# Layer norms: VectorE adds the scaled residual into PSUM sums that are still open

## The reference, cut to what matters

```
h = layer_norm(ALPHA * h + mix(h))     # mix: an SSD mixer (layer 0), latent attention (layer 1)
h = layer_norm(ALPHA * h + conv_ffn(h))
layer_norm(x) = (x - mean) * rsqrt(var + 1e-5) * g + b
```

## Time and profile before

| what | us |
|---|---|
| median of 3 runs (lowest, highest) | 1258.52 (1258.48, 1260.17) |
| span of the profiled execution | 1257.2 |
| TensorE busy in it | 1242.1 |
| VectorE busy in it | 932.5 |
| ScalarE busy in it | 684.2 |

### The profile page before, as it was taken

One profiled execution on the slowest core, in us unless ns is written; L12 is line 12 of the kernel. 1 busy time (PEld: TensorE's weight loads), 2 busy tenths in 40 slices (PEclk: granted clock), 3 DMA queues, 4 the chain that ended last, 5 costly groups with the idle time before them and its releaser, 6 DMA issues. The chain is left out here.

```text
span 1257.2 us, 18334 instructions
## 1 busy us (share of the span) xinstructions
PE 1242.1 (99%) x7514; PEld 1102.9 (88%) x7514; DVE 932.5 (74%) x1292; ACT 684.2 (54%) x872; POOL 68.2 (5%) x93
## 2 busy tenths in 40 slices
PE   9999999999999999999999999999999999999997
PEld 8878999989988888889998888888888888888886
DVE  6676857875456666577997998788888868788877
ACT  6654444343553444455777655466655574566652
POOL 2000000100000000000003331000000000000000
PEclk9999999999999999999999999999999999999999
DMA  9664545656435665647656654655554744655551
GB/s 294 219 184 144 185 143 188 214 186 209 168 101 170 199 194 178 197 138 219 185 168 210 203 191 151 217 185 201 184 186 138 231 134 134 201 194 179 197 194 41
DMA packets 162595, 227.97 MB, mean 181 GB/s; under 512 B 7853, under 2 KB 123825, under 8 KB 162384
## 3 DMA queue, kind: packets, MB, share of 16 engines
q1 hardware_dynamic: 159392, 216.68, 53.5%
q0 software_dynamic: 2816, 9.52, 2.3%
q10 hardware_dynamic: 304, 0.59, 0.1%
HBM read 225.68 MB, written 1.10 MB: 180 GB/s over the span
## 5 line engine op out<-in xcount | busy, mean ns | idle before, releaser
L1310 DVE TENSOR_TENSOR wlo<-raw,whi 128x2048 fp32r<-128x2048 f32 (+3 forms) x185 | 415.9, 2260 | 113.9 <-ACT whi L830 112.8
L830 ACT ACTIVATE whi<-raw 128x2048 fp32r<-128x2048 f32 (+3 forms) x185 | 345.9, 1883 | 16.0 <-DMA raw<-in_w_xkv 6.1
L2159 PE MATMUL psum<-h_both,whi 128*128 128x512 f32 x714 | 254.7, 396 | 0.0
L2158 PE MATMUL psum<-h_both,wlo 128*128 128x256 f32 x714 | 199.4, 279 | 0.3 <-DVE h_both L1364 0.3
L2125 PE MATMUL psum<-h_both,whi 128*128 128x256 f32 x688 | 195.9, 285 | 0.0
L2127 PE MATMUL psum<-h_both,wlo 128*128 128x256 f32 x688 | 194.6, 283 | 0.0
L2126 PE MATMUL psum<-h_both,whi 128*128 128x256 f32 x688 | 194.6, 283 | 0.0
L2125 PE MATMUL psum<-whi,r_hi 128*128 128x512 f32 x446 | 176.6, 396 | 0.0
L2127 PE MATMUL psum<-whi,r_lo 128*128 128x512 f32 x446 | 173.9, 390 | 0.0
L2126 PE MATMUL psum<-wlo,r_hi 128*128 128x512 f32 x446 | 173.8, 390 | 0.0
L2159 PEld LDWEIGHTS psum<-h_both,whi 128*128 128x128 f32 x714 | 134.0, 188 | 27.6
(11 more groups left out here) (350 smaller groups left out, 1807.1 us busy)
## 6 DMA issues: line engine op xcount, KB each, us to landing
raw<-in_ffn_up SPq DMA_DIRECT2D x40, 1024.0 KB, 5.1
raw<-in_w_in SPq DMA_DIRECT2D x31, 1024.0 KB, 5.8
raw<-in_ssd_in_proj SPq DMA_DIRECT2D x22, 1024.0 KB, 5.4
raw<-in_ffn_down SPq DMA_DIRECT2D x22, 1024.0 KB, 4.9
raw<-in_w_up SPq DMA_DIRECT2D x16, 1024.0 KB, 5.6
raw<-in_w_down SPq DMA_DIRECT2D x16, 1024.0 KB, 4.9
raw<-in_w_xkv SPq DMA_DIRECT2D x8, 1024.0 KB, 5.2
raw<-in_ssd_out_proj SPq DMA_DIRECT2D x8, 1024.0 KB, 5.2
```

The lines of the kernel that those rows point to most:

```text
L830: A(whi[u % SLOTS][:, 0:kt * n], raw[u % SLOTS][:, 0:kt * n], ACT.Copy).then_inc(hi_split, 1)
L1310: V.tensor_tensor(wlo[s][:, 0:kt * n], raw[s][:, 0:kt * n], whi[s][:, 0:kt * n].bitcast(F32), ALU.subtract).then_inc(lo_split, 1)
L2158: M(b[:, 0:T], w_lo_k, h_hi[:, k, :], start=False, stop=False)
L2159: return M(b[:, :], w_hi_k, h_both[:, :, k, :], start=False, stop=k == kt - 1)
```

## The change

The addition `ALPHA * xn` leaves the layer norm and becomes `add_residual`, which VectorE runs on a bank whose sum is not finished. TensorE waits for it (new semaphore `residual_in`) before it adds further to that bank.

- `so`: VectorE adds into the two banks of c0 once unit `so` (2, 0) has been used, then clears the pads of the feed-forward, then adds into those of c1 once `so` (2, 1) has been used. This stands after its last half of `lo` in the SSD part. TensorE waits in `last_two`, ahead of each bank's twelve matmuls.
- both feed-forwards: in group 9, after `ffn_taps` of half x, VectorE adds into the two banks of tile t = x, once fd 7 has been used. TensorE waits in fd 8, ahead of each bank.
- `ao`: VectorE adds c0 after step 9 of attention and a `lo`, c1 after step 10. TensorE waits in `last_two`.
- the flags `stop` of the units ahead are set, since VectorE touches the bank between; the later matmuls go on without `start`.

The core of the diff:

```diff
+            def add_residual(name, unit, places):
+                dve.wait_ge(unit_used, at[unit] + 1)
+                for c, t in places:
+                    b = bank[use[name(c, t)][0]][:, :]
+                    V.scalar_tensor_tensor(b, xn[:, t, halves[c]], ALPHA, b, ALU.mult, ALU.add).then_inc(residual_in, 1)
...
                     if rms:
                         chain(V.scalar_tensor_tensor(b, b, inv_ms[:, t:t + 1], x_, ALU.mult, ALU.add))
-                    else:
-                        chain(V.scalar_tensor_tensor(b, x_, alpha, b, ALU.mult, ALU.add))
                     mark(V.bn_stats(bn[:, t, c, :], b))
...
             for i in range(2):
                 lo_half(i)
+            so_sum = lambda c, t: ("so", c, t)
+            add_residual(so_sum, ("so", 2, 0), [(0, 0), (0, 1)])
...
                         ffn_taps(layer, g, x)
+                        if g == FFN_GROUPS - 2:
+                            add_residual(lambda c, t: ("ffn", layer, c, t), ("fd", layer, FFN_GROUPS - 4), [(0, x), (1, x)])
...
             ffn_pads()
+            add_residual(so_sum, ("so", 2, 1), [(1, 0), (1, 1)])
             lo()
-            layer_norm(lambda c, t: ("so", c, t), 3, lo_name="h5")
+            layer_norm(so_sum, 3, lo_name="h5")
...
             attend(9)
             lo()
+            add_residual(ao_sum, ("ao", 0, 0), [(0, 0), (0, 1)])
             attend(10)
+            add_residual(ao_sum, ("ao", 0, 1), [(1, 0), (1, 1)])
...
+            def residual_after(n):
+                pe.wait_ge(residual_in, residuals[0] + n)
...
+            def residual_first(inner):
+                def before(t, c, k):
+                    if k == 0:
+                        residual_after(2 * c + t + 1)
+                    inner(t, c, k)
+                return before
...
-                            last_two([at[("so", q, c)] for c in range(2)], r_hi, r_lo, 4, so_banks, first_tile("h5"))
+                            last_two([at[("so", q, c)] for c in range(2)], r_hi, r_lo, 4, so_banks, residual_first(first_tile("h5")))
...
-                        wide_unit(at[("fd", layer, g)], r_hi, r_lo, 2 * (g % 4), banks, g == 0, False)
+                        wide_unit(at[("fd", layer, g)], r_hi, r_lo, 2 * (g % 4), banks, g == 0, g == FFN_GROUPS - 4,
+                                  before=(lambda t, c: residual_after(2 * t + c + 1)) if g == FFN_GROUPS - 3 else None)
```

More of the change, by code:

```diff
@@ L620, in build @@
         low_out = sem("low_out")
+        residual_in = sem("residual_in")
         dt_sum, dt_log, dta_ready, cum_row = sem("dt_sum"), sem("dt_log"), sem("dta_ready"), sem("cum_row")
@@ L1446, in residual, with layer_norm @@
                             after_tile()
-            def layer_norm(name, uses, alpha=ALPHA, lo_name=None, rms=False, piece=None):
+            def add_residual(name, unit, places):
[3 more added lines that the diff above has]
+                    V.scalar_tensor_tensor(b, xn[:, t, halves[c]], ALPHA, b, ALU.mult, ALU.add).then_inc(residual_in, 1)
+            def layer_norm(name, uses, lo_name=None, rms=False, piece=None):
                 def add(c, t):
@@ L2098, in _ @@
             lo()
+            ao_sum = lambda c, t: ("ao", c, t)
+            add_residual(ao_sum, ("ao", 0, 0), [(0, 0), (0, 1)])
             attend(10)
+            add_residual(ao_sum, ("ao", 0, 1), [(1, 0), (1, 1)])
             lo()
@@ L2102, in _ @@
             ffn_pads()
-            layer_norm(lambda c, t: ("ao", c, t), 5, lo_name="h7")
+            layer_norm(ao_sum, 5, lo_name="h7")
             ffn(1)
@@ L2110, in _ @@
             M = nc.tensor.matmul
-            halves_normed = [0]
+            halves_normed, residuals = [0], [0]
+            def residual_after(n):
+                pe.wait_ge(residual_in, residuals[0] + n)
             def claim(key):
@@ L2121, in fill, with three @@
                 return filled[use[key][0]]
[L2123 to L2127, removed]
+            def three(o, a_hi, a_lo, b_hi, b_lo, start, stop_, resumed=False):
+                M(o, a_hi, b_hi, start=start, stop=False, skip_group_check=resumed)
+                M(o, a_hi, b_lo, start=False, stop=False, skip_group_check=resumed)
+                return M(o, a_lo, b_hi, start=False, stop=stop_, skip_group_check=resumed)
             def weights(u):
@@ L2187, in a_unit, with wide_unit @@
                 last.then_inc(unit_used, 1)
-            def wide_unit(u, x_hi_, x_lo_, tile0, banks, first, final, summed=False):
+            def wide_unit(u, x_hi_, x_lo_, tile0, banks, first, final, summed=False, before=None):
                 w_hi, w_lo, kt, _ = weights(u)
@@ L2193, in wide_unit @@
                     for c in range(2):
+                        if before is not None:
+                            before(t, c)
                         for k in range(kt):
@@ L2196, in wide_unit @@
                             last = three(banks[c][t][:, :], x_hi_[:, tile0 + k, ts], x_lo_[:, tile0 + k, ts], w_hi[:, k, cs], w_lo[:, k, cs],
-                                         first and k == 0, final and k == kt - 1)
+                                         first and k == 0, final and k == kt - 1, before is not None)
                         if summed and (t, c) != (NT - 1, 1):
@@ L2211, in last_two, with last_two_wide @@
                             last = three(banks[c][t][:, :], x_hi_[:, tile0 + k, ts], x_lo_[:, tile0 + k, ts], w_hi[:, k, :], w_lo[:, k, :],
-                                         False, k == kt - 1)
+                                         False, k == kt - 1, True)
                         last.then_inc(bank_summed if t == 0 else unit_used, 1)
-            def last_two_wide(us, ready, x_hi_, x_lo_, tiles, banks, before):
+            def last_two_wide(us, ready, x_hi_, x_lo_, tiles, banks, before, resumed):
                 for t in range(NT):
@@ L2227, in last_two_wide @@
                                 last = three(banks[c][t][:, :], x_hi_[:, tiles[i] + k, ts], x_lo_[:, tiles[i] + k, ts], w_hi[:, k, cs], w_lo[:, k, cs],
-                                             False, (i, k) == (1, kt - 1))
+                                             False, (i, k) == (1, kt - 1), resumed)
                             if (t, c, i) == (1, 1, 0):
@@ L2581, in _ @@
             last_two_wide([at[("down", g)] for g in pair], lambda i: pe.wait_ge(up_lo, pair[i] + 1), r_hi, r_lo,
-                          [2 * (g % 3) for g in pair], mlp_banks, first_tile("h4"))
+                          [2 * (g % 3) for g in pair], mlp_banks, first_tile("h4"), False)
             def lead(name, us, first_key, back_keys):
@@ L2768, in _ @@
                         if k == 0:
-                            last_two([at[("so", q, c)] for c in range(2)], r_hi, r_lo, 4, so_banks, first_tile("h5"))
+                            last_two([at[("so", q, c)] for c in range(2)], r_hi, r_lo, 4, so_banks, residual_first(first_tile("h5")))
                         continue
-                    a_unit(at[("so", q, k)], r_hi, r_lo, 4 * (q % 2), so_banks[k], q == 0, False,
+                    a_unit(at[("so", q, k)], r_hi, r_lo, 4 * (q % 2), so_banks[k], q == 0, q == 2,
                            between=lambda n: ssd_step(SSD_PER_UNIT * u + n))
@@ L2791, in ffn @@
                         pe.wait_ge(f_lo, 11 * layer + g + 1)
-                        wide_unit(at[("fd", layer, g)], r_hi, r_lo, 2 * (g % 4), banks, g == 0, False)
+                        wide_unit(at[("fd", layer, g)], r_hi, r_lo, 2 * (g % 4), banks, g == 0, g == FFN_GROUPS - 4,
+                                  before=(lambda t, c: residual_after(2 * t + c + 1)) if g == FFN_GROUPS - 3 else None)
+                residuals[0] += 4
                 pair = (FFN_GROUPS - 2, FFN_GROUPS - 1)
                 last_two_wide([at[("fd", layer, g)] for g in pair], lambda i: pe.wait_ge(f_lo, 11 * layer + pair[i] + 1), r_hi, r_lo,
-                              [2 * (g % 4) for g in pair], banks, before_last)
+                              [2 * (g % 4) for g in pair], banks, before_last, True)
+            residuals[0] += 4
             ffn(0, "h5", first_tile("h6"))
@@ L2949, in attend_at @@
                 return between
+            ao_before = residual_first(first_tile("h7"))
             def before_second(t, c, k):
@@ L2953, in before_second @@
                     wait_drained(pe, ("mo", 2 + k // 2))
-                first_tile("h7")(t, c, k)
+                ao_before(t, c, k)
             ao = [[claim(("ao", c, t)) for t in range(NT)] for c in range(2)]
-            a_unit(at[("ao", 0, 0)], r_hi, r_lo, 4, ao[0], True, False, ready=mo_ready, between=attend_at(7))
-            a_unit(at[("ao", 0, 1)], r_hi, r_lo, 4, ao[1], True, False, between=attend_at(9))
+            a_unit(at[("ao", 0, 0)], r_hi, r_lo, 4, ao[0], True, True, ready=mo_ready, between=attend_at(7))
+            a_unit(at[("ao", 0, 1)], r_hi, r_lo, 4, ao[1], True, True, between=attend_at(9))
```

(1 more changed line is left out.)

## The result

The changed kernel takes 1262.26 us (median of 20 runs, 1260.57 to 1264.0); the kernel before, on the same chip, 1258.89 (1258.25 to 1260.9). The ratio is 1.0022 with a 95% interval of 1.0016 to 1.0029: slower, by 3.4 us in the medians. The forecast was 1261.3, with a range of 1258.9 to 1264.0.

A forecast was written before the change was run, and what follows sets the result against it. TensorE was taken as the bound, VectorE mattering only where TensorE waits and at the end. Net terms +1.77 (h5), +1.69 (h6), -0.56 (h7), -0.17 (feed-forward 1, end) gave 1258.52 + 2.73 = 1261.3 us, range 1258.9 to 1264.0.

The forecast's parts named there:

- the sum: Net over the whole kernel, 1.77 + 1.69 - 0.56 - 0.17 = +2.73 us, giving 1261.3 us.
- three signs of being wrong: No TensorE stop at `so`, a pause in feed-forward 0 under 2 us, or a clock fall behind a pause.
- What bounds the kernel: TensorE, busy 1242.1 of 1257.2 us; VectorE's work counts only where TensorE waits for it and at the end.
- Part 1: Additions leaving the four layer norms win 0.58 us in h5, 0.83 in h6, 0.56 in h7, 1.02 at the end.
- Part 2: At `so`, TensorE pauses 2.35 us before the first bank of `last_two`; h5 nets +1.77 us.
- Part 3: In feed-forward 0, four additions delay `r_lo` of group 10 by 2.64 us; TensorE pauses 2.52, h6 nets +1.69.
- Part 4: At `ao`, the additions fall into VectorE's idle time and add nothing; h7 nets -0.56 us.
- Part 5: In feed-forward 1, TensorE pauses 0.85 us for `r_lo` of group 10; with 1.02 gained at the end, nets -0.17.
- rival C: Twelve matmuls behind each of two long pauses run at 1.2 GHz, 2.7 us more each: +8.1, 1266.7 us; chance 0.06.
- Rivals B and D: B: VectorE absorbs the additions, -2.99 us, 1255.5, chance 0.06. D: one long pause fails to come, 1258.8, chance 0.16.

The follow-up runs named there:

- e3: Kernel before with the change at `ao` only, additions elsewhere left in the layer norm; 1258.33 us, ratio 0.9995.
- e5: Changed kernel with all four additions of `so` ahead of VectorE's last two halves of `lo`; 1259.98 us.
- e8: Changed kernel with `so` additions ahead of the last two `lo` halves and feed-forward additions in groups 5 and 7, ahead of the taps; 1256.32 us.
- e6: Changed kernel with the feed-forwards' additions moved to groups 5 and 7, behind the taps; 1265.60 us, ratio 1.0051.
- e9: e8 with the c0 additions of `so` between VectorE's last two halves of `lo`; 1257.38 us, ratio 0.9988.
- e2: Kernel before with the change in the two feed-forwards only; 1259.86 us, ratio 1.0007.
- e4: Changed kernel with the two c0 additions of `so` between VectorE's last two halves of `lo`; 1259.83 us.
- e1: Kernel before with the change at `so` only; 1262.15 us, ratio 1.0022.
- e10: Changed kernel with only the feed-forwards' additions moved, to groups 5 and 7 ahead of the taps; 1260.02 us, ratio 1.0007.
- e7: Changed kernel with `so` additions ahead of the last two `lo` halves and feed-forward additions in groups 5 and 7, behind the taps; 1261.82 us, ratio 1.0018.

## Why the prediction was right, and where its terms were off

The direction was right, and so was the mechanism of the pauses. That the size came so near, +3.4 where the sum said +2.7, is in part luck. The nine executions without a fall of the clock are at +2.0 and the eleven with one at +4.0; the sum lies between the two, too high by its pairs of additions and too low by the fall that it left out. Two of the prediction's three signs of being wrong also came true: the pause of feed-forward 0 is under 2 us (+1.9 by the shift), and the clock fell behind a pause.

- **What bounds the kernel; a pause of TensorE is the price.** Right. But for the eight matmuls at the low clock and the end, every difference between the traces is a place where TensorE waits or no longer waits for VectorE. The additions themselves are as many as before (VectorE busy 932.5 and 930.7 us).
- **Part 1, what is removed.** Right for h6 (-0.84; 1.02 less three quarters of 0.227 is 0.85, where the sum took 0.83) and the end (-1.05, forecast -1.02). For h5 and h7 the transposes stopped waiting as said (-0.56 and -0.55), but 0.37 came back at once in each: the matmul behind the last transpose needs the low part of the third transposed half, and TensorE, now earlier, waits for that. In the trace of the changed kernel the last transpose of h5 begins at 799.21 and the next matmul 0.99 later, of which 0.37 is new by the comparison above. The profile puts the wait down to "issue"; that it is for VectorE's low part is read from the times: VectorE's row begins at 799.40 and lasts 0.69, so it ends 0.11 before the matmul starts. I had asked what is late next after the first stall and not after the second. e3 shows the same steps at h7, alone.

```profile
799.21 0.60 PE L2259 MATMUL psum<-cst,xn 128*128 128x128 f32 x4
799.40 0.69 DVE L1345 TENSOR_TENSOR h_both<-psum,h_both 128x512 fp32r<-128x512 f32 x1 [0.47 <-ACT h_both L847]
800.20 0.47 PE L2143 MATMUL psum<-whi,h_both 128*128 128x512 f32 x1 [0.39 <-issue]
```

- **Part 2, `so`.** The pause was right to 0.01 us. e5 shows that it is only the place in VectorE's queue: the same four additions, begun 2.3 us earlier against TensorE's time, cost less than 0.2 us.
- **Part 3, feed-forward 0.** Mechanism right, size off: `r_lo` of group 10 came 2.10 us later relative to TensorE's time, not 2.64. An addition moves what follows by less than its length. With the first pair of additions behind the taps the next `lo` begins 2.91 us after the taps' start (948.21 to 951.12), before 1.80 (944.43 to 946.23): 1.11 for the pair. With the second pair the product begins 2.91 after the taps' start (955.29 to 958.20), before 1.90 (950.41 to 952.31): 1.01. Together they are 2.12, where I had put 2.64.
- **Part 4, `ao`.** Right in that TensorE waits for nothing there; -0.35 instead of -0.56, for the reason given under part 1.
- **Part 5, feed-forward 1.** Pause 0.41, not 0.85; the same mis-sized pairs, 2.12 instead of 2.64, account for the difference to within 0.1.
- **The clock, rival C at 0.06.** This is the term that the forecast left out. It is not a fixed price but a chance: the clock fell in eleven of the twenty runs (by their times and clocks), and it cost 1.7 us in the profiled one. Two errors partly cancelled: without a fall the change costs 1260.87 - 1258.89 = +2.0 us where the sum said +2.7; with one, +4.0. By the price that I had derived, 2.7 us for twelve matmuls, the fall was smaller, since only eight matmuls ran at the low level. The trace of before had been read too boldly: a clock of 1.00 between 5 and 10 us did not show that a pause is harmless, since the longest gap there is 1.2 us. Nor was it so that this trace shows no fall anywhere. Behind TensorE's last matmul the granted clock is 1.00 up to 1254 and 0.50 from there to the end, where no matmul pays for it; the window over this stretch has 0.78:

```profile
1249.90:1257.20 7.30, 0.04 (x1) 0.00 (x0) 4.76 (x9) 0.00 (x0) 0.54 (x1) 0.78 0.38 144
```

The rule of the Trainium skill (TensorE: Matmul & The Clock Gate, Why this matters for your kernels) that idle gaps between bursts throttle TensorE was the better guide. These traces bear it out in kind but not in length: the gaps that it warns of are longer than the two here, TensorE's wait of 2.2 us at `so` and of 1.8 in feed-forward 0, so read strictly it would have let both pass.

- **Rivals B and D** are out for the changed kernel: both long pauses came.

The numbers leave +2.0 (no fall) against a sum of the measured steps of about +2.2; that 0.2 is within what single executions scatter (before: 1258.25 to 1260.9).

One question stays open: why the clock falls behind a pause in some executions and not in others. All that the runs show is the count for each kind of pause. These counts go by the two groups of times; the mean clock alone can't tell a fall, since it also takes in the low stretch at the end, and 0.998 stands with quick runs too (1256.03 in e8). With 17 of 98 runs of the kernel before in an upper group, some upper runs of the other kernels may also have another cause than their pause.

## What to carry to other kernels

- Moving work to an engine's idle time needs two checks at the new place: what stands behind it in that engine's queue, and when the other engine asks for the result. Here the same sixteen additions cost +3.4 us in one arrangement, +6.8 in another (e6) and won 2.5 in a third (e8).
- If the consumer's next step lies right behind the step from which the producer's queue is fed, nothing put behind that point in the queue can be in time; put it ahead.
- A pause of the matrix engine can cost more than its length, and only some of the executions show it. Look at the times and the granted clock of every run, not at one profile.

## What the runs showed of the hardware

- With no long pause (e8) or one of 1.2 us (e9) none of eleven runs is in an upper group. With the pause of about 2.0 us in feed-forward 0 and none above 1.2 elsewhere, three of eleven (e2), four of eleven (e4) and seven of eleven (e5) are; this is read from times and clocks, and no kept trace shows the low clock there. With one of 2.4 at `so` it is seven of eight (e1) and eight of eleven (e10).
- The traces show a fall behind the pause at `so` (the changed kernel, e1, e6, e10) and behind that at fd 4 (e7 twice, e6 once). Each low stretch lasts 3.4 us, and the matmuls in it start 0.43 us apart.
- The fall needn't come at the end of the pause: in e7 the pause ends at 882.23 and the matmuls slow down from 883.6; in e10 the clock is low from 778.9 and TensorE goes on at 779.11.
- An f32 addition of 128 x 512 into PSUM lasts 0.69 us by its row; two in a row take 1.28, and where `lo` follows, it begins 1.2 after the first.
